# An encoder block on eight cores: x read transposed, 1/rms applied behind the projections, mixing and feed-forward over all 1024 tokens at once

## The chip, the cores and the metric

The kernel runs on all eight cores of one Trainium2 chip. Each core works alone on 1024 of the 8192 tokens, with its own copy of every weight, and the cores never exchange anything. The metric is the device time of the slowest core, in microseconds (us). A core has a matrix engine (TensorE, PE in the rows; PEld is its weight load), a vector engine (VectorE, DVE), an activation engine (ScalarE, ACT), GpSimd (POOL) and SyncE (SP). In this kernel POOL and SP only issue transfers: POOL those that turn f32 weights into bf16 on the way, SP the plain ones. Sixteen DMA engines move the bytes of both queues.

## The reference

```python
h = rms_norm(x, norm1_pre)                       # x: (2, 4096, 2048) f32
z = h @ w_in                                     # 2048 -> 7168: [u 1024 | v 1024 | p 1024 | ga 2048 | gb 2048]
u, v = gelu(z[u]), gelu(z[v]);  p = z[p]
y_a = u * (W_s @ layer_norm(v) + b)              # 8 heads, 128x128 matrix per block of 128 tokens
y_b = group_linear(trailing_mean(p, 2/4/8/16) - p) * scale     # needs 16 tokens of p before the first one
merged = sigmoid(ga) * (y_a @ w_a_out) + sigmoid(gb) * (y_b @ w_b_out)
x = x + rms_norm(merged @ w_mix_out, norm1_post)
h = rms_norm(x, norm2_pre)
x = x + rms_norm((silu(h @ w_ffn_gate) * (h @ w_ffn_up)) @ w_ffn_down, norm2_post)   # inner width 5632
```

## The kernel before

`Sched.add` records every operation with the bytes that it reads and writes; `analyze` and `emit` turn that into semaphore waits. Each engine runs its operations strictly in the order in which the program adds them, so the order of the code is the order of every queue. One byte array `arena` is the whole of SBUF, and buffers share addresses by hand. PSUM is eight banks of 128x512 f32; `nb()` hands them out in a circle. All matmuls are bf16, mostly 128x128 weights against 512 columns.

`stage_AB` takes the 1024 tokens once. Nine row tiles of x (16 halo tokens, then eight of 128) are loaded, squared and summed (L386), scaled by 1/rms (L395), transposed on PE (L349) and copied out of PSUM with the gain (L358, L362) into `hT`. Then come, each from `hT`:

- p (L448 halo, L460), eight chunks of 128 channels, evicted by ScalarE (L465); VectorE forms the trailing sums by one to four shifted adds of some 1039 columns (L475) and the mean minus the token (L482);
- v (L509), token tile by token tile, GELU (L514), layer norm on VectorE (L516 to L533), each tile with a square root on ScalarE;
- the pool's group linear (L549, evicted at L556), u with the 128x128 mixing (L572, L585), and the two gates with the two output projections (L623 to L632), 48 matmuls for each 128 output channels and 512 tokens, gathered in `mergedT`.

`stage_CDE(hf)` then runs twice, once for each half of 512 tokens:

- C: `mergedT @ w_mix` (L692), root mean square norm and residual (L738), second norm, transposes (L349 again) into `h2T`; the first three feed-forward slices run in halves of 256 columns between them (L766, L769);
- D: for each of 44 slices of 128 inner channels 16 + 16 matmuls (L807, L810), SiLU (L815) and product (L817), with a ring of three weight buffers of 1 MB;
- E: four blocks of 512 output channels, 44 x 4 matmuls each (L846), squares and gain (L855, L859); behind the fourth block all four token tiles are normed, added to x (L738) and stored (L866).

So `w_mix`, `w_gu` and `w_dn` are loaded twice, once for each half:

```python
        stage_AB()
        if last_stage in (None, "C", "D", "E"):
            for hf in range(nhalves):
                stat_ctr[0] = 128
                stage_CDE(hf)
```

Of the kernel before, what the change touches and what calls it, by code (L numbers as in the profile page):

```python
# [190 lines left out]
class Arena:  # L191
    def __init__(self, ap):
        self.ap = ap
        self.ptr = 0

    def alloc(self, nbytes, dtype, pattern=None, **kw):
        off = (self.ptr + GRAN - 1) // GRAN * GRAN if nbytes >= GRAN else (self.ptr + 31) // 32 * 32
        self.ptr = off + nbytes
# [4 lines left out]
        return v

def build_program(dbg=None, nhalves=2, last_stage=None):
    nc = bass.Bass("TRN2", target_bir_lowering=False)
# [31 lines left out]

    sems = []
    import contextlib  # L240
    with contextlib.ExitStack() as es:
# [4 lines left out]

# [32 lines left out]
        def dma(eng, out, in_, group=None, after=()):  # L279
            return S.add(eng, lambda e, o=out, i=in_: e.dma_start(out=o, in_=i),  # L280
                         reads=[in_], writes=[out], dma=True, group=group, after=after)

        def emit_consts(first_x_load):
            dma("sp", ident, ident_d, group="c0")
            dma("sp", g1T, g1T_d, group="c0")
            dma("sp", g2T, g2T_d, group="c0")
            dma("sp", pscT, pscT_d, group="c0")
            dma("sp", invf, invf_d, group="c0")
            dma("pool", sgwT, sgwT_d, after=[first_x_load])
            dma("pool", wpool, w_pool)  # L290
            S.add("dve", lambda e: e.memset(sgwT[64:128, :, 0:64], 0.0), reads=[], writes=[sgwT])
# [699 lines left out]
```

How the kernel before makes its waits and increments, by code:

```python
        def run(engname, e):  # L172
            waited = {}
            for op in per_eng.get(engname, []):
                need = {}
                for d in op.deps:
                    dop = self.ops[d]
                    if need.get(dop.sem, 0) < dop.sigval:
                        need[dop.sem] = dop.sigval
                for s, v in need.items():
                    if waited.get(s, 0) < v:
                        e.wait_ge(semh[s], v)
                        waited[s] = v
                if op.fn is None:
                    continue
                ins = op.fn(e)
                if op.signal:
                    ins.then_inc(semh[op.sem], 16 if op.dma else 1)
```

## Time and profile before

| | |
|---|---|
| median of 6 runs | 1733.83 us (1731.96 to 1734.46) |
| the profiled execution: its time | 1732.88 us |
| its span (slowest core, 5) | 1731.3 us |
| spans of the eight cores | 1718.7 to 1731.3 us |
| mean granted TensorE clock of the cores | 0.969 to 0.972 of full speed |
| PE busy | 1579.7 us, 91% |
| VectorE, ScalarE busy | 360.5 us (21%), 273.3 us (16%) |
| moved by the DMA engines | 226.14 MB, mean 131 GB/s |

The span runs from the first to the last instruction of a core; the profiled execution took 1.6 us more than its span. Busy shares are means over stages of very different kinds. DMA figures count the bytes that the transfers write; a weight that is cast on the way is read as twice as many bytes from HBM.

### The profile page before, as it was taken

What the parts mean: (1) busy time and instruction counts of PE and PEld (TensorE: products, weight loads), DVE (VectorE), ACT (ScalarE), POOL (GpSimd) and SP (SyncE); (2) the same over time, 40 slices, a digit from 0 to 9 for tenths busy, and PEclk for the clock granted to TensorE, in tenths of its full rate; (3) what the DMA queues carried; (4) which work ended last, traced back from release to release, by engine and by line L of the source; (5) the groups of instructions that cost most, each with busy time, mean ns of one, the idle gap of its engine ahead of it and who ended that gap; (6) DMA issues with size and microseconds to landing.
All of it is one profiled execution on the core that took longest, in us unless ns stands there. A gap on an engine that the chain in (4) does not pass through costs nothing.

```text
span 1731.3 us, 19473 instructions; the slowest of 8 cores (1718.7 to 1731.3 us)
## 1 busy us (share of the span) xinstructions
PE 1579.7 (91%) x7728; PEld 746.2 (43%) x7728; DVE 360.5 (21%) x654; ACT 273.3 (16%) x585; POOL 122.7 (7%) x234
## 2 busy tenths in 40 slices
PE   2699899999999986999999999986499999999994
PEld 1344344444444435444444444432344444444442
DVE  4366431112111233000100000041500110010003
ACT  6314411111111133000000000020400000000001
POOL 0000000000000000000000111100000000011110
PEclk9999999999999997999999999997789999999997
DMA  8950164444448760998899899999188888879992
GB/s 209 189 100 1 25 107 82 80 80 79 74 73 151 144 131 14 162 153 154 151 152 153 150 173 169 165 182 226 42 129 154 155 149 153 155 150 167 176 162 106
DMA packets 39258, 226.14 MB, mean 131 GB/s; under 512 B 4848, under 2 KB 6896, under 8 KB 21360
## 3 DMA queue, kind: packets, MB, share of 16 engines
q0 software_dynamic: 34528, 197.93, 68.1%
q1 hardware_dynamic: 4640, 26.96, 4.6%
q8 instruction: 63, 1.03, 0.2%
q14 instruction: 27, 0.22, 0.0%
HBM read 410.21 MB, written 8.39 MB: 242 GB/s over the span
## 4 chain that ended last, share of the span: by engine, by line
PE 85%; DMA 8%; DVE 3%; issue 2%; ACT 2%; DVEq 0%; POOL 0%; ACTq 0%; SPq 0%; POOLq 0%
PE psum L846 17%; PE psum L807 16%; PE psum L810 16%; PE psum L623 6%; PE psum L626 6%; DMA arena<-x_ext 4%; PE psum L460 3%; PE psum L692 3%; PE psum L509 3%; PE psum L632 3%; PE psum L629 3%; PE psum L572 3%; DMA out<-arena 1%; DMA arena<-w_dn 1%; PE psum L766 1%
## 5 line engine op out<-in xcount | busy, mean ns | idle before, releaser
L807 PE MATMUL psum<-arena 128*128 128x512 bf16 x1312 | 298.9, 381 | 8.0 <-DMA arena<-w_gu 8.0
L846 PE MATMUL psum<-arena 128*128 128x512 bf16 x1408 | 304.6, 379 | 1.4 <-DMA arena<-w_dn 1.3
L810 PE MATMUL psum<-arena 128*128 128x512 bf16 x1312 | 296.6, 379 | 0.0
L846 PEld LDWEIGHTS psum<-arena 128*128 128x128 bf16 x1408 | 137.3, 98 | 168.7 <-issue 4.0
L807 PEld LDWEIGHTS psum<-arena 128*128 128x128 bf16 x1312 | 128.9, 98 | 164.5 <-issue 11.8
L810 PEld LDWEIGHTS psum<-arena 128*128 128x128 bf16 x1312 | 128.3, 98 | 154.8
L817 DVE TENSOR_TENSOR arena<-arena,psum 128x512 bf16<-128x512 f32 x82 | 56.4, 688 | 521.5 <-ACT arena L815 521.5
L692 PE MATMUL psum<-arena 128*128 128x512 bf16 x512 | 112.7, 383 | 21.7 <-DMA arena<-w_mix 21.7
L815 ACT ACTIVATE arena<-psum 128x512 f32<-128x512 f32 x82 | 49.0, 597 | 528.5 <-PE psum L810 528.5
L623 PE MATMUL psum<-arena 128*128 128x512 bf16 x512 | 115.7, 379 | 0.9 <-DVE arena L592 0.9
L626 PE MATMUL psum<-arena 128*128 128x512 bf16 x512 | 115.7, 379 | 0.0
L349 PE MATMUL psum<-arena 128*128 128x128 bf16 (+1 forms) x272 | 27.3, 280 | 83.2 <-DVE arena L395 28.7
L280 POOL DMA_DIRECT2D arena<-w_gu x88 | 46.5, 529 | 715.4 <-PE psum L810 495.4
L692 PEld LDWEIGHTS psum<-arena 128*128 128x128 bf16 x512 | 50.5, 99 | 83.6 <-issue 24.5
L859 DVE TENSOR_TENSOR arena<-psum,arena 128x512 f32<-128x512 f32 x32 | 19.9, 683 | 289.7 <-ACT arena L855 289.7
L642 DVE TENSOR_TENSOR arena<-arena,psum 128x512 f32<-128x512 f32 x32 | 22.0, 688 | 267.1 <-ACT arena L638 267.1
L623 PEld LDWEIGHTS psum<-arena 128*128 128x128 bf16 x512 | 50.0, 98 | 61.3 <-issue 1.1
L626 PEld LDWEIGHTS psum<-arena 128*128 128x128 bf16 x512 | 50.1, 98 | 60.4
L855 ACT ACTIVATE arena<-psum 128x512 bf16<-128x512 f32 x32 | 18.6, 597 | 290.2 <-PE psum L846 290.2
L280 POOL DMA_DIRECT2D arena<-w_dn x88 | 46.5, 530 | 251.2 <-PE psum L846 211.5
L638 ACT ACTIVATE arena<-psum 128x512 f32<-128x512 f32 x32 | 19.1, 597 | 286.2 <-PE psum L632 286.2
L349 PEld LDWEIGHTS psum<-arena 128*128 128x128 bf16 (+1 forms) x272 | 23.8, 130 | 86.6 <-issue 86.5
(81 smaller groups left out, 1052.1 us busy)
## 6 DMA issues: line engine op xcount, KB each, us to landing
arena<-w_gu POOLq DMA_DIRECT2D x88, 1024.0 KB, 9.8
arena<-w_dn POOLq DMA_DIRECT2D x88, 512.0 KB, 11.3
arena<-w_gab POOLq DMA_DIRECT2D x16, 1536.0 KB, 12.9
arena<-x_ext SPq DMA_DIRECT2D x16, 1024.0 KB, 9.8
arena<-w_mix POOLq DMA_DIRECT2D x8, 2048.0 KB, 30.6
out<-arena SPq DMA_DIRECT2D x8, 1024.0 KB, 14.2
arena<-w_p POOLq DMA_DIRECT2D x8, 512.0 KB, 12.6
arena<-w_v POOLq DMA_DIRECT2D x2, 2048.0 KB, 24.9
```

Of the source, the lines that this page charges most:

```text
L280: return S.add(eng, lambda e, o=out, i=in_: e.dma_start(out=o, in_=i), reads=[in_], writes=[out], dma=True, group=group, after=after)
L460: ins = e.matmul(PS(b1), lhsT=slot[:, kc, :], rhs=hT[:, kc, hf * HT:(hf + 1) * HT], start=(kc == 0), stop=(kc == 15))
L509: ins = e.matmul(PS(b), lhsT=hT[:, kc, tb * 128:(tb + 1) * 128], rhs=Wv[:, ct, kc, :], start=(kc == 0), stop=(kc == 15))
L572: ins = e.matmul(PS(b1), lhsT=slot[:, kc, :], rhs=hT[:, kc, hf * HT:(hf + 1) * HT], start=(kc == 0), stop=(kc == 15))
L623: ins = e.matmul(PS(bs[0]), lhsT=slot[:, kc, :], rhs=hT[:, kc, tk], start=(kc == 0), stop=(kc == 15))
L626: ins = e.matmul(PS(bs[1]), lhsT=slot[:, 16 + kc, :], rhs=hT[:, kc, tk], start=(kc == 0), stop=(kc == 15))
L629: ins = e.matmul(PS(bs[2]), lhsT=slot[:, 32 + kc, :], rhs=yAT[:, kc, tk], start=(kc == 0), stop=(kc == 7))
L692: ins = e.matmul(PS(b), lhsT=mergedT[:, kc, tk0 + tb * 128: tk0 + (tb + 1) * 128], rhs=slot[:, kc, :], start=(kc == 0), stop=(kc == 15))
L807: ins = e.matmul(PS(b1), lhsT=slot[:, kc, :], rhs=h2T[:, kc, :], start=(kc == 0), stop=(kc == 15))
L810: ins = e.matmul(PS(b2), lhsT=slot[:, 16 + kc, :], rhs=h2T[:, kc, :], start=(kc == 0), stop=(kc == 15))
L817: S.add("dve", lambda e, b2=b2, o=sgj, f=f: e.tensor_tensor(out=hidT[:, f, :], in0=o, in1=PS(b2), op=ALU.mult), reads=[sgj, PS(b2)], write ...
L846: ins = e.matmul(PS(banks[tb]), lhsT=hidT[:, fc, tb * 128:(tb + 1) * 128], rhs=slot[:, fl, :], start=(fc == 0), stop=(fc == NFC - 1))
```

## The change

x is no longer transposed on PE. The host hands it over as `xTa` (512 tokens) and `xTb` (the other 512 and, last, the 16 halo tokens) in channel-major form, beside the plain `x` for the residual. `x_chunk` loads 128 channels, multiplies them by the gain into `xg` (bf16, not normed), squares them on ScalarE into one buffer `sq`, and adds them on VectorE to `acc`. The mean over channels is a matmul: `tok_rstd` gives 1/rms for each token of a tile as a column (for v, as the scale of the GELU), and three f32 matmuls with `ones` give it as a row on all partitions (`rsb`), by which VectorE multiplies every result of p, u and the gates as it leaves PSUM.

The order becomes v, p, u with the pool's linear between the heads, gates. v runs first, chunk by chunk as `w_v` (now 16 loads of 128 channels) and x arrive; the second half of x is processed between the evictions of the first half's v.

C, D and E run once over 1024 tokens: all of `w_mix` stays in four buffers, each `w_gu` slice serves two groups of 512 columns out of a ring of five, and each `w_dn` piece serves all eight token tiles out of a ring of eleven, with one PSUM bank for each tile. x after the first sub-layer goes to DRAM (`x1_d`) and comes back for the last residual. E's last block runs tile by tile, so that each tile is normed and stored as it ends.

The core of the diff:

```diff
+        def x_chunk(half, kc):
+            n = HT if half == 0 else HT + HALO
+            t = xr[(half * 16 + kc) % NXR][:, 0:n]
+            dma("sp", t, (xTa_d if half == 0 else xTb_d)[kc], after=[w_ops[12]] if (half, kc) == (1, 0) else ())
+            ts(xg[:, kc, xcols[half]], t, g1T[:, kc:kc + 1], ALU.mult)
+            a = acc[:, xcols[half]]
+            if kc == 0:
+                act(AF.Square, a, t)
+            else:
+                for lo in range(0, n, HT):
+                    hi = min(lo + HT, n)
+                    act(AF.Square, sq[:, 0:hi - lo], t[:, lo:hi])
+                    tt(a[:, lo:hi], a[:, lo:hi], sq[:, 0:hi - lo], ALU.add)
...
+        def v_mm(tb, ct, kcs):
+            b = (tb % 4) * 2 + ct
+            tk = slice(tb * 128, (tb + 1) * 128)
...
+        def tok_rstd(half, b):
+            pe([(PS(b)[:, i:i + 1], acc[:, half * HT + i * 128: half * HT + (i + 1) * 128], one1, True, True)
+                for i in range(4)], [acc[:, half * HT:(half + 1) * HT], one1], [b])
+            r4 = rt[:, half * 4:half * 4 + 4]
+            ts(r4, PS(b)[:, 0:4], EPS, ALU.add)
+            act(AF.Sqrt, r4, r4)
+            recip(r4)
...
+        def v_evac(tb, ct):
+            b = (tb % 4) * 2 + ct
+            d = vg[tb][:, ct * 512:(ct + 1) * 512]
+            act(AF.Gelu, d, PS(b), scale=rt[:, tb:tb + 1])
...
+        def v_norm_r(half):
+            r4 = lnr[:, half * 4:half * 4 + 4]
+            act(AF.Sqrt, r4, r4)
+            recip(r4)
...
+        def v_norm(tb):
+            v = vg[tb]
+            ts(v, v, mvs[:, tb * 2:tb * 2 + 1], ALU.subtract, lnr[:, tb:tb + 1], ALU.mult)
+            tt(v, v, lng, ALU.mult)
+            tt(v_ln[:, tb, :], v, lnb, ALU.add)
...
+        KA, KE = 12, 4
+        late = list(range(KA, 16))
+        for kc in range(16):
+            x_chunk(0, kc)
+        order = [(tb, ct) for tb in range(4) for ct in range(2)]
+        for kc in range(KA):
+            for tb, ct in order[:7]:
+                v_mm(tb, ct, [kc])
+        for tb, ct in order[:2]:
+            v_mm(tb, ct, late)
+        tok_rstd(0, 7)
+        for tb, ct in order[2:7]:
+            v_mm(tb, ct, late)
+        v_mm(3, 1, list(range(16)))
+        for i, (tb, ct) in enumerate(order):
+            v_evac(tb, ct)
+            if i >= 1:
+                x_chunk(1, i - 1)
+        dma("sp", lng, lng_d, group="ln")
+        dma("sp", lnb, lnb_d, group="ln")
+        v_norm_r(0)
+        for kc in range(7, 16):
+            x_chunk(1, kc)
+            if kc >= 12:
+                v_norm(kc - 12)
...
+        order = [(tb, ct) for tb in range(4, 8) for ct in range(2)]
+        for tb, ct in order[:7]:
+            v_mm(tb, ct, list(range(KE)))
+        for kc in range(KE, KA):
+            for tb, ct in order[:7]:
+                v_mm(tb, ct, [kc])
+        tok_rstd(1, 7)
+        for tb, ct in order[:7]:
+            v_mm(tb, ct, late)
+            v_evac(tb, ct)
+        SEG = [(0, 347), (347, 694), (694, NT)]
+        bbs = [0, 1, 2]
+        for b, (lo, hi) in zip(bbs, SEG):
+            pe([(PS(b)[:, 0:hi - lo], ones, acc[:, lo:hi], True, True)], [ones, acc[:, lo:hi]], [b])
+        v_mm(7, 1, list(range(16)))
+        for b, (lo, hi) in zip(bbs, SEG):
+            ts(rsb[:, lo:hi], PS(b)[:, 0:hi - lo], EPS, ALU.add)
+        v_evac(7, 1)
+        act(AF.Sqrt, rsb, rsb)
+        recip(rsb)
+        v_norm_r(1)
+        bank_ctr[0] = 3
+
...
+        for i, c in enumerate(pcs):
+            g = c // 2
+            w = 2 << g
+            slot = pslots[i]
+            pj = pTs[i % 2]
+            for lo, hi in SEG:
+                b = nb()
+                pe([(PS(b)[:, 0:hi - lo], slot[:, kc, :], xg[:, kc, lo:hi], kc == 0, kc == 15) for kc in range(16)],
+                   [slot, xg[:, :, lo:hi]], [b])
+                hi_t = min(hi, TOK)
+                tt(pj[:, HALO + lo:HALO + hi_t], PS(b)[:, 0:hi_t - lo], rsb[:, lo:hi_t], ALU.mult)
+                if hi > TOK:
+                    tt(pj[:, 0:HALO], PS(b)[:, TOK - lo:hi - lo], rsb[:, TOK:NT], ALU.mult)
...
+            cur, lo, step, bi = pj, 0, 1, 0
+            while step < w:
+                nlo = lo + step
+                dst = sAB[bi]
+                tt(dst[:, nlo:NT], cur[:, nlo:NT], cur[:, nlo - step:NT - step], ALU.add)
+                cur, lo, step, bi = dst, nlo, step * 2, bi ^ 1
+            stt(pooledT[:, c, :], cur[:, HALO:], 1.0 / w, pj[:, HALO:], ALU.mult, ALU.subtract)
+            tt(t16, cur[:, HALO:2 * HALO], invf[:, g, :], ALU.mult)
+            tt(pooledT[:, c, 0:HALO], t16, pj[:, HALO:2 * HALO], ALU.subtract)
+            if norm_q:
+                v_norm(norm_q.pop(0))
...
+        def gab_load(d):
+            dma("pool", ringB[d % 3], w_gab[d])
...
+                tt(u_, PS(b1), rsb[:, tk], ALU.mult)
+                act(AF.Gelu, u_, u_)
...
+                tt(yAT[:, h, tk], t_, u_, ALU.mult)
...
+        for d in range(16):
...
+                for b, t_ in ((bs[0], sa[hf]), (bs[1], sb[hf])):
+                    tt(t_, PS(b), rsb[:, tk], ALU.mult)
+                    act(AF.Sigmoid, t_, t_)
+                tt(sa[hf], sa[hf], PS(bs[2]), ALU.mult)
+                tt(sb[hf], sb[hf], PS(bs[3]), ALU.mult)
+                tt(mergedT[:, d, tk], sa[hf], sb[hf], ALU.add)
+            if d + 3 < 16:
+                gab_load(d + 3)
+            if d in (0, 2, 4):
+                dma("pool", Wmix[d // 2], w_mix[d // 2])
+            if d == 13:
+                dma("pool", Wmix[3], w_mix[3])
+
...
+        dma("sp", xt[0], x_d[0:128, :])
...
+        for f in range(3):
+            dma("pool", ringD[f], w_gu[f])
...
+        def rstd_col(dst, src):
+            ts(dst, src, 1.0 / D, ALU.mult, EPS, ALU.add)
+            act(AF.Sqrt, dst, dst)
+            recip(dst)
...
+        def c_mm(tb, et):
+            b = nb()
+            tk = slice(tb * 128, (tb + 1) * 128)
+            pe([(PS(b), mergedT[:, kc, tk], Wmix[et][:, kc, :], kc == 0, kc == 15) for kc in range(16)],
+               [mergedT[:, :, tk], Wmix[et]], [b])
+            cols = slice(et * 512, (et + 1) * 512)
+            act(AF.Square, junk, PS(b), accum=cpart[tb % 2][:, et:et + 1])
+            tt(mo[:, cols], PS(b), gp1[:, cols], ALU.mult)
+
+        def c_chain(tb):
+            x_, r_ = xt[tb % 2], cs[tb % 2]
+            sum4(r_[:, 0:1], cpart[tb % 2])
+            rstd_col(r_[:, 1:2], r_[:, 0:1])
+            stt(x_, mo, r_[:, 1:2], x_, ALU.mult, ALU.add)
...
+            dma("sp", x1_d[rows, :], x_, writes=[("dram", "x1", tb)])
+            act(AF.Square, xb[tb % 2], x_, accum=r_[:, 2:3])
+            rstd_col(r_[:, 3:4], r_[:, 2:3])
+            stt(xb[tb % 2], x_, r_[:, 3:4], g2, ALU.mult, ALU.mult)
+            if tb + 2 < 8:
+                dma("sp", x_, x_d[(tb + 2) * 128:(tb + 3) * 128, :])
...
+        def c_tr(tb):
...
+                S.add("pe", tr, reads=[xb[tb % 2], ident], writes=[PS(b)])
+                dst = h2T[:, half * 8:half * 8 + 8, tb * 128:(tb + 1) * 128]
+                src = pb.rearrange("p (c n) -> p c n", c=8)
...
+        for tb in range(8):
...
+                c_mm(tb, et)
+                if et == 1 and tb >= 2:
+                    c_tr(tb - 2)
+            c_chain(tb)
...
+        def d_mm(f, hf):
+            slot = ringD[f % NRD]
+            tk = slice(hf * HT, (hf + 1) * HT)
+            b1, b2 = nb(), nb()
+            for b, k0 in ((b1, 0), (b2, 16)):
+                pe([(PS(b), slot[:, k0 + kc, :], h2T[:, kc, tk], kc == 0, kc == 15) for kc in range(16)],
+                   [slot, h2T[:, :, tk]], [b])
+            return f, tk, b1, b2
...
+        def d_ev(f, tk, b1, b2):
+            s_ = sg[sgc[0] % 2]
+            sgc[0] += 1
+            act(AF.Silu, s_, PS(b1))
+            tt(hidT[:, f, tk], s_, PS(b2), ALU.mult)
...
+        def d_load(f):
+            dma("pool", ringD[f % NRD], w_gu[f])
...
+        pend = [d_mm(0, 0)]
+        c_tr(6)
+        pend.append(d_mm(1, 0))
+        pend.append(d_mm(2, 0))
+        d_ev(*pend.pop(0))
+        c_tr(7)
+        for p_ in pend:
+            d_ev(*p_)
+        d_load(3)
+        d_load(4)
+        for f in range(3):
+            d_ev(*d_mm(f, 1))
+            d_load(f + 5)
+        for f in range(3, NFC):
+            for hf in range(2):
+                d_ev(*d_mm(f, hf))
+            if f + 5 < NFC:
+                d_load(f + 5)
...
+        def e_load(i):
+            et, fg = eslots[i]
+            dma("pool", ringE[i % NRE], w_dn[et, fg])
...
+        for et in range(3):
+            cols = slice(et * 512, (et + 1) * 512)
+            for fg in range(11):
...
+                for tb in range(8):
+                    tk = slice(tb * 128, (tb + 1) * 128)
+                    pe([(PS(tb), hidT[:, fg * 4 + fl, tk], slot[:, fl, :], fg == 0 and fl == 0, fg == 10 and fl == 3)
+                        for fl in range(4)], [hidT[:, fg * 4:fg * 4 + 4, tk], slot], [tb])
+                    if fg == 10:
+                        act(AF.Square, junkE, PS(tb), accum=epart[tb][:, et:et + 1])
+                        tt(fo[:, tb, cols], PS(tb), gp2[:, cols], ALU.mult)
+                e_load(i + NRE)
+        for tb in range(8):
...
+            for fg in range(11):
+                slot = ringE[(33 + fg) % NRE]
...
+            act(AF.Square, junkE, PS(tb), accum=epart[tb][:, 3:4])
+            r_, x_ = es_[tb % 2], x1t[tb % 2]
...
+            rstd_col(r_[:, 1:2], r_[:, 0:1])
...
+            stt(x_[:, 0:512], f4, r_[:, 1:2], x_[:, 0:512], ALU.mult, ALU.add)
+            stt(f4, PS(tb), r_[:, 1:2], gp2[:, 1536:2048], ALU.mult, ALU.mult)
+            tt(x_[:, 1536:2048], f4, x_[:, 1536:2048], ALU.add)
+            stt(x_[:, 512:1536], fo[:, tb, 512:1536], r_[:, 1:2], x_[:, 512:1536], ALU.mult, ALU.add)
+            dma("sp", out_d[rows, :], x_, writes=[("dram", "out", tb)])
+            if tb + 2 < 8:
+                nrows = slice((tb + 2) * 128, (tb + 3) * 128)
+                dma("sp", x_, x1_d[nrows, :], reads=[("dram", "x1", tb + 2)])
```

## Rows read from the trace of the kernel before

**Rows 1.** The page's first line: span and slowest core.

```profile
span 1731.3 us, 19473 instructions; the slowest of 8 cores (1718.7 to 1731.3 us)
```

**Rows 2.** Timeline of PE: start, us, engine, line, instructions, idle before.

```profile
1239.16 1.91 PE L766 MATMUL psum<-arena 128*128 128x256 bf16 x16
1240.91 1.91 PE L769 MATMUL psum<-arena 128*128 128x256 bf16 x16
...
1246.15 1.06 PE L349 MATMUL psum<-arena 128*128 128x128 bf16 x16
...
1270.71 5.98 PE L807 MATMUL psum<-arena 128*128 128x512 bf16 x16 [4.10 <-DMA arena<-w_gu]
...
1556.98 152.11 PE L846 MATMUL psum<-arena 128*128 128x512 bf16 x704 [0.56 <-DMA arena<-w_dn]
```

**Rows 3.** Stretches: busy us of each engine, granted clock, DMA share, GB/s.

```profile
0.00:64.00 64.00, 15.39 (x147) 13.70 (x148) 26.73 (x92) 37.22 (x95) 4.58 (x12) 1.00 0.90 207
...
179.00:194.00 15.00, 9.78 (x33) 3.39 (x31) 8.41 (x12) 11.65 (x19) 0.00 (x0) 0.77 0.00 0
...
254.00:585.70 331.70, 331.53 (x1537) 150.33 (x1538) 62.02 (x95) 34.94 (x63) 11.15 (x21) 1.00 0.52 89
...
641.00:697.00 56.00, 31.20 (x257) 25.72 (x256) 22.73 (x59) 21.57 (x55) 1.59 (x3) 0.76 0.14 23
697.00:983.00 286.00, 285.37 (x1322) 129.29 (x1323) 28.21 (x41) 24.48 (x41) 23.58 (x45) 1.00 0.90 154
983.00:1134.00 151.00, 150.56 (x698) 67.77 (x696) 7.45 (x12) 7.26 (x24) 23.60 (x44) 1.00 1.02 168
...
1160.00:1215.00 55.00, 31.07 (x136) 13.36 (x133) 8.65 (x17) 6.69 (x21) 0.00 (x0) 0.81 0.99 229
1215.00:1271.00 56.00, 31.79 (x257) 26.06 (x258) 22.49 (x59) 20.62 (x53) 1.58 (x3) 0.74 0.19 38
...
1709.00:1731.30 22.30, 0.08 (x1) 0.00 (x0) 13.02 (x20) 4.51 (x13) 0.00 (x0) 0.58 0.46 188
```

**Rows 4.** DMA issues: KB each, median us to landing.

```profile
arena<-w_gu POOLq DMA_DIRECT2D x88, 1024.0 KB, 9.8
```

**Rows 5.** VectorE's groups by form: busy us, mean ns, idle before.

```profile
L738 DVE SCALAR_TENSOR_TENSOR arena<-arena 128x2048 f32<-128x2048 f32 x16 | 37.0, 2344 | 3.3 <-DMA arena<-x_ext 3.3
...
L642 DVE TENSOR_TENSOR arena<-arena,psum 128x512 f32<-128x512 f32 x32 | 22.0, 688 | 267.1 <-ACT arena L638 267.1
...
L516 DVE BATCH_NORM_STATS2 arena<-arena 128x6 f32<-128x512 f32 x16 | 10.2, 682 | 0.0
...
L395 DVE TENSOR_SCALAR arena<-arena 128x2048 bf16<-128x2048 f32 x8 | 10.2, 1278 | 0.0
L475 DVE TENSOR_TENSOR arena<-arena 128x1039 f32<-128x1039 f32 x8 | 9.9, 1242 | 25.9 <-ACT arena L465 25.9
...
L527 DVE TENSOR_SCALAR arena<-arena 128x1024 f32<-128x1024 f32 x8 | 6.5, 812 | 0.9
...
L333 DVE TENSOR_SCALAR arena<-arena 128x1 f32<-128x1 f32 x32 | 4.8, 149 | 6.0 <-ACT arena L386 5.2
```

**Rows 6.** ScalarE's groups by form, same columns.

```profile
L702 ACT ACTIVATE arena<-psum 128x512 bf16<-128x512 f32 x32 | 19.0, 596 | 92.2 <-PE psum L692 92.2
...
L744 ACT ACTIVATE arena<-arena 128x2048 bf16<-128x2048 f32 x8 | 15.2, 1898 | 0.2
L514 ACT ACT_TABLE_LOAD x8 | 10.3, 1283 | 1.1 <-PE psum L509 0.9
```

**Rows 7.** Timeline of one square root between two VectorE instructions.

```profile
637.95 0.15 DVE L333 TENSOR_SCALAR arena<-arena 128x1 f32<-128x1 f32 x1
638.19 0.20 ACT L336 ACTIVATE arena<-arena 128x1 f32<-128x1 f32 x1 [3.21 <-DVE arena L333]
...
638.49 0.16 DVE L338 RECIPROCAL arena<-arena 128x1 f32<-128x1 f32 x1 [0.40 <-ACT arena L336]
```

**Rows 8.** Timeline of SyncE's last DMA issues.

```profile
1719.63 7.11 SPq L866 DMA_DIRECT2D out<-arena  x4
```

More of the change, by code:

```diff
@@ L23 @@
 ARENA_BYTES = 212736
+NT = HALO + TOK
 GRAN = 256
@@ new lines, in build_program @@
+        acc = at(Z3 + 18 * KB + 512, F32, NT)
+        ones = at(Z3 + 23 * KB, F32, 128)
+        Z4 = Z3 + 24 * KB
+        sgwT = at(Z4, BF16, 8, 128)
+        wpool = at(Z4 + 2 * KB, BF16, 4, 2, 256)
+        sq = at(Z4 + 6 * KB, F32, HT)
+        sa = [at(Z4 + 2 * i * KB, F32, HT) for i in range(2)]
+        sb = [at(Z4 + (4 + 2 * i) * KB, F32, HT) for i in range(2)]
+        rsb = at(Z4 + 8 * KB, F32, NT)
+        Z5 = Z1 + 38 * KB
+        xt = [at(Z1 + (8 + 8 * i) * KB, F32, D) for i in range(2)]
@@ L277, in st @@
             return stat[:, o:o + n]
[L279 to L291, printed above, removed]
@@ new lines, in ts, with tt @@
+        def ts(out, in0, s1, op0, s2=None, op1=None):
+            kw = {} if op1 is None else {"op1": op1}
+            rd = [in0] + [s for s in (s1, s2) if hasattr(s, "tensor")]
+            return S.add("dve", lambda e: e.tensor_scalar(out=out, in0=in0, scalar1=s1, scalar2=s2, op0=op0, **kw),
+                         reads=rd, writes=[out])
+        def tt(out, a, b, op, eng="dve"):
+            return S.add(eng, lambda e: e.tensor_tensor(out=out, in0=a, in1=b, op=op),
+                         reads=[a, b], writes=[out])
@@ new lines, in pe, with fn @@
+        def pe(mms, reads, banks):
+            def fn(e):
+                ins = None
+                for o, l, r, s_, t_ in mms:
+                    ins = e.matmul(o, lhsT=l, rhs=r, start=s_, stop=t_)
+                return ins
+            return S.add("pe", fn, reads=reads, writes=[PS(b) for b in banks])
+        rt = st(8)
+        mvs = st(16)
+        lnr = st(8)
+        bst = [st(12) for _ in range(4)]
+        xcols = [slice(0, HT), slice(HT, NT)]
+        dma("act", g1T, g1T_d)
+        S.add("dve", lambda e: e.memset(ones, 1.0 / D), writes=[ones])
@@ new lines, in build_program @@
+        S.add("dve", lambda e: e.memset(one1, 1.0 / D), writes=[one1])
+        w_ops = [dma("pool", Wv[:, kc, :], w_v[kc]) for kc in range(16)]
+        def x_chunk(half, kc):
[11 more added lines that the diff above has]
+                    tt(a[:, lo:hi], a[:, lo:hi], sq[:, 0:hi - lo], ALU.add)
@@ new lines, in build_program, with wtile @@
+        v_norm_r(0)
[3 more added lines that the diff above has]
+                v_norm(kc - 12)
+        dma("sp", ident, ident_d, group="c1")
+        dma("sp", pscT, pscT_d, group="c1")
+        dma("sp", invf, invf_d, group="c1")
+        ra = [0]
+        def wtile(src):
+            slot = ringA[ra[0] % 4]
+            ra[0] += 1
+            dma("pool", slot, src)
+            return slot
+        pcs = [7, 6, 5, 4, 3, 2, 1, 0]
+        pslots = [wtile(w_p[c]) for c in pcs[:4]]
@@ new lines, in build_program @@
+        eslots = [(et, fg) for et in range(4) for fg in range(11)]
+        def e_load(i):
+            et, fg = eslots[i]
+            dma("pool", ringE[i % NRE], w_dn[et, fg])
+        for i in range(NRE):
+            e_load(i)
+        dma("sp", gp2, gp2_d)
+        epart = [st(4) for _ in range(8)]
+        es_ = [st(2) for _ in range(2)]
+        for tb in range(2):
+            rows = slice(tb * 128, (tb + 1) * 128)
+            dma("sp", x1t[tb], x1_d[rows, :], reads=[("dram", "x1", tb)])
```

768 lines of the change are left out of this document (187 added, 581 removed).

## The prediction

> **What bounds the kernel now.** The first line gives the span, 1731.3 us, and the slowest core [rows 1]. I read PE's timeline next. Where PE runs without a break, 704 matmuls of 512 columns take 152.11 us [rows 2]: 0.216 us each. Counted from the code, the program has 7072 such matmuls (v, p and u 256 each, the pool 32, gates and output projections 1536, C 512, D 2816, E 1408), 1528 us at that pace. So 203 us of the span are something else, and the table of stretches shows where [rows 3]. In the first 64 us PE works 15.4 us, on transposes. In 179 to 194 it is a third idle, waiting for the pool's evictions. In each half's stretch between C and D (641 to 697, 1215 to 1271) it works 31 to 32 of 56 us, and the DMA engines stand almost still: the chain of norms is the limit there. In 1160 to 1215 it works 31 of 55 us with the DMA engines at 0.99: the second half's `w_mix` and x. In the last 22.3 us it works not at all. In the long stretches it is full (331.53 of 331.70, 285.37 of 286.00) at a granted clock of 1.00. The bound is PE, and what can be won is the 203 us around it.
>
> **The second loads of the weights.** D and E load 154 and 168 GB/s with the DMA engines at 0.90 and 1.02 [rows 3], and yet PE loses 0.6 us in the 286 of D. The traffic that goes is hidden today, so halving it is worth nothing in these stretches. D's cover even grows: a slice feeds 64 matmuls, 13.8 us, against 9.8 us to land [rows 4].
>
> **PE's work after the change.**
> - v: 256 x 0.216 = 55.3 us.
> - p: 3 x 16 matmuls of 346 or 347 columns for each of 8 chunks. 16 of 256 columns take 1.75 us (two starts in [rows 2]), 0.109 each; between that and 0.216 a matmul of 347 costs 0.147: 8 x 48 x 0.147 = 56.6 us.
> - u and pool: 288 x 0.216 = 62.2, and 16 groups of four 128-column mixings at 0.066 (16 transposes in 1.06 us [rows 2]), 4.2: 66.4 us.
> - gates 331.8, C 110.6, D 608.3, E 304.1 us; eight tiles' transposes (16 each) 8.5 us.
> Together 1541.6 us. No transposes for the first norm, no halo matmuls.
>
> **The start, until v is done.** `w_v` and the first half of x are 4.19 MB each. At 168 GB/s (E's casts) and 229 GB/s (1160 to 1215) [rows 3] they take 25.0 + 18.3 us on the shared engines; from 2 us on, the last chunk lands at 45. Both at 229 it is 39, both at 168 it is 52. PE uses each chunk as it lands and is not the limit. What follows is a chain through VectorE, which runs in program order:
> - Chunk 15 squared (0.60, [rows 6]), added (0.69), four f32 matmuls (not in the trace; 0.6 taken, hundredths at the least), 1/rms with two handovers of 0.1 (the square root leaves VectorE idle 0.40 for 0.20 of work, [rows 7]), GELU's table load 1.28 and the first GELU 0.60 [rows 6]: 49.8.
> - Then evictions of v and chunks of the second half take turns. A chunk's gain costs 0.43 (between 0.149 for 1 column and 1.278 for 2048, [rows 5]), its adds 0.69 and 0.17. With `bn_stats` 0.68 and the aggregates that is 2.2 us a step. But `sq` is one buffer and 528 columns are two squares, so ScalarE may not write the 16-column square before the first add has read, nor the next chunk's before the second add. A step is then 16-column square 0.2, GELU 0.6, `bn_stats`, aggregates and gain 1.3, add 0.69 and three handovers: 3.1 us. Seven steps and the first `bn_stats`: 22.4, to 72.2.
> - Layer norm's root with a table load, VectorE waiting: 1.9. Chunks 7 to 11 at 2.06 (0.60, 0.69, 0.20, 0.17 and four handovers): 10.3. Chunks 12 to 15 at 1.7, with three `v_norm` of 0.81 + 2 x 1.24 between them [rows 5], under which the next square hides: 16.7. `acc` is complete at 101.1.
> - `tok_rstd(1)` stands ahead of the remaining matmuls in PE's queue, so PE waits for all this. Then 0.6, 28 matmuls 6.1, 2.5 for the half-rate clock after the idle (16 matmuls took 5.98 us instead of 3.46, [rows 2]), the three `ones` matmuls 0.9 (0.4 at full clock), and the last tile's 16 matmuls 3.5: v ends at 114.7.
> That is 59.4 us of loss, against 64 now. If the handovers on `sq` cost nothing it is 12 less.
>
> **p and u.** VectorE now evicts p: for each chunk 3 x 0.51 and the halo 0.18, the shifted adds at 1.24 [rows 5], the mean 1.24, two small ones 0.35, and `v_norm` 3.29 behind the first four. Wide windows first: 2 x 11.5 + 2 x 10.2 + 2 x 5.8 + 2 x 4.5 = 64.0 us against PE's 56.6. Ahead of it stands the row form of 1/rms, PE already running: GELU 0.7, table load 1.28, root 1.0, reciprocal of 1040 columns. That is not in the trace: at least an add's 1.24; at most 15.7, if the 15 ns by which a reciprocal of one column exceeds a `tensor_scalar` of one [rows 5, 7] were for each column. I take 1.24, since a one-column instruction is nearly all fixed cost. PE may run eight banks, 18.8 us, ahead; followed bank by bank it waits 3.0 us near the end of p, and 15.9 with the long reciprocal. In the Trainium skill, "VectorE: DVE Perf Modes", section "Walkthrough: the 8-slice pipeline in each mode", reciprocal repeats its divide step 8 times. As an estimate from that page it would take 8.7 us here and the sum would rise by 6 us; no run here shows it.
> In u VectorE has 6 x 0.69 = 4.1 us for each head against PE's 8.3, so it catches up. The gates add two multiplies to each group: 5 x 0.69 = 3.4 us against 48 matmuls, 10.4 us. These cost nothing; the cover is PE's own work, three times as long.
>
> **C, D, E.** For each tile VectorE has four evictions 2.8, two short roots 2.0, the residual and the scaling 2.34 each [rows 5], a wait for ScalarE's square of x 2.3 [rows 6], and the transposes' copy, 1.2: 12.9 us against PE's 13.8 + 1.06. It keeps up, and the eight banks bridge its latency. The plain x loads and x1 stores are 1 MB a tile each way, 4.6 us each at 229 GB/s, in 14.9. Around the last transposes (tile 7's behind three feed-forward groups) PE waits for one copy and a handover: 1.5. Changes of banks and late `w_dn` pieces in E: 1.5. At the end only one tile is left: square and root 2.0, four VectorE steps 3.3, the store from issue to end 4.6 (the last one now leaves at 1726.7, [rows 1, 8]): 10 instead of 22.3.
>
> **The sum.** 114.7 + (1541.6 - 55.3) + 3.0 + 1.5 + 1.5 + 10 = 1617.0 us of span. Cross-check by what goes: start 4.6, halo 3, pool 8, the stretches around C some 86, the tail 12: 114 off 1731.3. The profiled execution took 1.6 more than its span, 1732.9, and the median of the runs is 1.0 above that: **1620 us**.
>
> **Rivals.**
> - The handovers at the start are cheaper, or the loads faster: 1620 - 12 = 1608, and 6 less with the early landing, 1602. For it: only VectorE's own time is a floor. Against: one `sq`.
> - VectorE's queue is longer than its rows: the long reciprocal (+13) and the late landing (+7): 1640. For it: p's 64.0 against 56.6 leaves no room. Against: the eight banks.
> - C does not keep up: `mo` and the chain are one buffer deep for eight tiles, and 12.9 stands against 14.9. If the chain's 10 us behind a tile's last matmul were exposed half, 8 x 5 more: 1660.
> - Slower than before: the clock. Today PE's full stretches are broken up; afterwards it is full for some 1490 us. If the granted level fell to half, a matmul would cost 0.21 us more, and 540 of them, a stretch of 230 us at 1.2 GHz, use up the gain: 1734 and beyond. Against it: on all eight cores 331.7, 286 and 151 us went by at 1.00 [rows 3], and the clock fell only behind PE's idle time. The Trainium skill, "TensorE: Matmul & The Clock Gate", Part 1, warns that dense matmuls on several cores of a die lower its clock; by that rule the whole sum would grow, and this trace does not agree.
>
> **Chances and range.** Forecast, 1610 to 1632: 0.55. Cheaper start: 0.17. Longer VectorE queue: 0.17. C not keeping up: 0.08. Clock: 0.03. The range 1600 to 1645 takes in the first three. Faster by more than 0.2% (what a measurement of this kernel can tell from no change): 0.96; within it 0.01; slower 0.03.
>
> **What would show it.** PE idle some 15 us before the f32 matmuls of the second half, released by VectorE's add; VectorE near full from 50 us to the end of p; gates starting near 240 us; no gap of more than 3 us from there to the end of E; the end 10 us behind PE's last matmul. Wrong: a gap in every tile of C, a granted clock under 0.95 in D, or v done before 95 or after 130 us.

## The result and the profile after

| | before | after |
|---|---|---|
| median of the runs, us | 1734.27 (20 runs) | 1632.37 (10 runs) |
| after / before | | 0.9416, 95% interval 0.9405 to 0.9427 |
| profiled execution, us | 1732.9 | 1630.6 |
| its span, us | 1731.3 | 1629.1 |

The times and ratios here and below are those of executions in which no die was held at a lower clock than the other (in the others the mean granted clock of a die's cores was as low as 0.81), except that the two medians are over all runs. Forecast were 1620 us and a span of 1617.0; the direction is right, the time lies in the range, and the span is 12.1 us above the sum. Most of what follows is about these 12 us.

The page of the changed kernel, first lines and busy times: PE's share is now 96%.

```profile
span 1629.1 us, 18914 instructions; the slowest of 8 cores (1625.4 to 1629.1 us)
...
PE 1559.5 (96%) x7414; PEld 721.8 (44%) x7414; DVE 453.0 (28%) x694; ACT 230.9 (14%) x438; POOL 75.3 (5%) x146
```

Its stretches, read as [rows 3]:

```profile
45.00:67.00 22.00, 14.73 (x52) 6.78 (x52) 7.72 (x20) 7.00 (x13) 0.00 (x0) 0.73 1.02 205
...
89.00:107.50 18.50, 0.12 (x1) 0.00 (x0) 15.65 (x23) 3.39 (x8) 0.00 (x0) 0.58 0.01 2
107.50:125.20 17.70, 17.63 (x80) 9.65 (x81) 10.69 (x24) 8.93 (x12) 0.00 (x0) 0.86 0.09 30
125.00:185.00 60.00, 51.27 (x324) 32.51 (x322) 53.71 (x63) 0.49 (x2) 3.28 (x7) 0.94 0.37 71
...
250.00:582.00 332.00, 332.00 (x1546) 150.74 (x1544) 111.21 (x163) 43.25 (x68) 9.50 (x18) 1.00 0.57 100
...
700.00:1313.00 613.00, 612.06 (x2861) 278.41 (x2859) 69.73 (x102) 59.32 (x99) 26.91 (x51) 1.00 0.45 86
1313.00:1617.00 304.00, 304.00 (x1410) 137.75 (x1408) 44.32 (x74) 24.01 (x70) 17.96 (x34) 1.00 0.47 102
1617.00:1629.10 12.10, 2.11 (x10) 0.78 (x8) 3.87 (x7) 0.89 (x3) 0.00 (x0) 0.81 0.35 143
```

From 250 us to the end of E, PE is idle for less than 1 us in all, at a granted clock of 1.00, the 2.4 GHz level: the gaps around C, between the halves and in the pool [rows 3] are gone. The DMA share in D and E is 0.45 and 0.47, where it was 0.90 and 1.02. What is left lies before 185 us and in the last 10.

PE's waits (us in total, times, longest), and PE's timeline at the start (start, us, ..., idle before and its releaser):

```profile
PE psum L365 <- DMA arena<-w_v: 23.6, 12, 8.6
PE psum L365 <- DMA arena<-invf: 18.4, 1, 18.4
PE psum L365 <- DVE arena L347: 8.7, 3, 3.7
PE psum L365 <- DVE arena L343: 7.9, 4, 6.8
PE psum L365 <- DVE arena L645: 0.9, 1, 0.9
```

```profile
45.65 14.73 PE L365 MATMUL psum<-arena 128*128 128x512 bf16 x52 [7.30 <-DMA arena<-w_v]
67.22 15.84 PE L365 MATMUL psum<-arena 128*128 128x512 bf16 x63 [6.84 <-DVE arena L343]
...
107.57 47.71 PE L365 MATMUL psum<-arena 128*128 128x1 f32 x282 [18.45 <-DMA arena<-invf]
158.33 7.24 PE L365 MATMUL psum<-arena 128*128 128x346 bf16 x48 [3.05 <-DVE arena L347]
169.25 8.92 PE L365 MATMUL psum<-arena 128*128 128x346 bf16 x48 [3.67 <-DVE arena L347]
```

The wait of 18.45 us is the one for 1/rms of the second half. It is put down to the load of `invf`, but that load only ended last: VectorE's final add into `acc`, in the timeline below, begins at 105.90. The three waits that follow, 8.7 us, are p's matmuls waiting for banks that VectorE has not evicted.

VectorE's timeline, same columns:

```profile
53.73 1.29 DVE L413 BATCH_NORM_STATS2 arena<-arena 128x6 f32<-128x512 f32 x2 [2.16 <-ACT arena L337]
...
60.49 0.49 DVE L343 TENSOR_SCALAR arena<-arena 128x528 bf16<-128x528 f32 x1 [3.85 <-PE psum L365]
...
105.90 0.17 DVE L347 TENSOR_TENSOR arena<-arena 128x16 f32<-128x16 f32 x1 [0.41 <-ACT arena L337]
```

And its groups by form in 125 to 205 us, the stretch of p (as [rows 5]):

```profile
L347 DVE TENSOR_TENSOR arena<-arena 128x1039 f32<-128x1039 f32 x8 | 9.9, 1242 | 1.0 <-DVE arena L347 0.3
L352 DVE SCALAR_TENSOR_TENSOR arena<-arena 128x1024 bf16<-128x1024 f32 x8 | 9.8, 1225 | 1.4 <-DVE arena L347 1.4
...
L356 DVE RECIPROCAL arena<-arena 128x1040 f32<-128x1040 f32 x1 | 6.7, 6654 | 1.1 <-ACT arena L337 1.1
```

The reciprocal of 1040 columns took 6.65 us, where the sum had 1.24.

### The profile page after: what moved, and what is told of

Read it like the earlier page. It is cut to its first block, busy times and chain, and to the rows that moved or that the text cites. A ratio compares the mean times of both kernels' runs of the same rounds, so it can differ in the third digit from the quotient of the medians.

```text
span 1629.1 us, 18914 instructions; the slowest of 8 cores (1625.4 to 1629.1 us)
## 1 busy us (share of the span) xinstructions
PE 1559.5 (96%) x7414; PEld 721.8 (44%) x7414; DVE 453.0 (28%) x694; ACT 230.9 (14%) x438; POOL 75.3 (5%) x146
## 4 chain that ended last, share of the span: by engine, by line
PE 91%; DVE 4%; DMA 2%; issue 1%; ACT 1%; POOL 0%; DVEq 0%; ACTq 0%; SPq 0%; POOLq 0%
PE psum L365 90%; DVE arena L347 3%; DMA arena<-w_v 2%; ACT arena L337 1%; DVE arena L343 1%; POOL arena L326 0%; PE psum L635 0%; DVE arena L352 0%; DVE arena L413 0%; DVEq L183 0%; DMA arena<-invf 0%; DVEq L748 0%; DVE arena L645 0%; DVE arena L416 0%; ACTq L183 0%
## 5 line engine op out<-in xcount | busy, mean ns | idle before, releaser
L365 PE MATMUL psum<-arena 128*128 128x512 bf16 (+2 forms) x7286 | 1553.5, 376 | 59.6 <-DMA arena<-w_v 23.6
L365 PEld LDWEIGHTS psum<-arena 128*128 128x128 bf16 x7286 | 714.2, 99 | 895.0 <-issue 80.6
L347 DVE TENSOR_TENSOR arena<-arena,psum 128x512 bf16<-128x512 f32 (+1 forms) x152 | 104.4, 687 | 594.8 <-PE psum L365 594.3
L347 DVE TENSOR_TENSOR arena<-psum,arena 128x512 f32<-128x512 f32 (+3 forms) x168 | 106.2, 640 | 415.2 <-PE psum L365 383.9
L337 ACT ACTIVATE arena<-psum 128x512 f32<-128x512 f32 (+1 forms) x152 | 90.6, 597 | 853.7 <-PE psum L365 852.4
L337 ACT ACTIVATE arena<-arena 128x512 f32<-128x512 f32 (+3 forms) x164 | 95.4, 584 | 432.7 <-DVE arena L347 354.1
L347 DVE TENSOR_TENSOR arena<-arena 128x512 bf16<-128x512 f32 (+8 forms) x153 | 109.2, 714 | 28.5 <-ACT arena L337 19.4
L352 DVE SCALAR_TENSOR_TENSOR arena<-arena 128x1024 bf16<-128x1024 f32 (+4 forms) x40 | 63.7, 1592 | 5.1 <-DVE arena L356 3.0
L326 POOL DMA_DIRECT2D arena<-w_gu x44 | 23.2, 528 | 675.6 <-PE psum L365 518.7
L343 DVE TENSOR_SCALAR arena<-arena 128x1 f32<-128x1 f32 (+3 forms) x72 | 26.9, 376 | 38.8 <-ACT arena L337 18.1
L356 DVE RECIPROCAL arena<-arena 128x1 f32<-128x1 f32 (+2 forms) x29 | 11.2, 388 | 15.4 <-ACT arena L337 15.4
L635 PEld LDWEIGHTS psum<-arena 128*128 128x128 bf16 x128 | 7.8, 98 | 1.9
```

Source lines behind the costliest of these rows:

```text
L326: return S.add(eng, lambda e: e.dma_start(out=out, in_=in_), reads=[in_] if reads is None else reads, writes=[out] if writes is None else ...
L337: return S.add("act", lambda e: e.activation(out=out, in_=in_, func=func, **kw), reads=rd, writes=[out] + ([accum] if accum is not None el ...
L343: return S.add("dve", lambda e: e.tensor_scalar(out=out, in0=in0, scalar1=s1, scalar2=s2, op0=op0, **kw), reads=rd, writes=[out])
L347: return S.add(eng, lambda e: e.tensor_tensor(out=out, in0=a, in1=b, op=op), reads=[a, b], writes=[out])
L352: return S.add("dve", lambda e: e.scalar_tensor_tensor(out=out, in0=in0, scalar=scalar, in1=in1, op0=op0, op1=op1), reads=rd, writes=[out])
L356: S.add("dve", lambda e: e.reciprocal(out=x_, in_=x_), reads=[x_], writes=[x_])
```

## The experiments

**Theory A**: from 50 us to the end of p, VectorE's queue (its work and its waits) is the bound. What leaves it, or a wait of its that goes, moves everything after it; what is only moved within it gives nothing. **Rival B**: only PE's wait for the second half's 1/rms costs; whatever brings that forward is a gain in full. Spans, each of the slowest core, are compared with 1629.1; the eight cores of that one execution differ by 3.7 us, so differences of 1 or 2 us are not read.

**e1: finer tracking of what instructions share.** The scheduler orders accesses by pieces of `GRAN` bytes. A row of `xg` has 2080 bytes, so the columns that VectorE writes for the second half share a piece with columns that PE still reads for the first: the 3.85 us at 60.49. `pscT`, `one1` and `g1T` share one too.

```diff
-GRAN = 256
+GRAN = 32
```

> Dependencies are tracked in pieces of 32 bytes instead of 256; nothing else changes. In the trace of the changed kernel VectorE stands still 3.9 us at 56.6 us until PE has ended the first half's last v matmuls (rows of xg are 2080 bytes apart, so the columns that VectorE writes and those that PE reads share a piece), and PE starts the f32 matmuls 1.5 us after the last add, behind three small transfers that share a piece with a constant. Theory A (VectorE's queue, waits included, sets the time from 50 us to the end of p): both waits go, 4 to 5 us less, 1627 us, ratio 0.997. Theory B (PE's wait for 1/rms of the second half alone costs, VectorE has slack in p): 5 us less at the end of v as well, so this run doesn't tell A from B. Theory C (the waits are cover for something else, as the landing of x): under 1 us.

Measured: 1627.1 to 1627.5 us in three executions and 1636.5 in a fourth (the changed kernel, too, has one of 1640.1 beside 1630.1 to 1634.0), ratio 0.9395 (0.9371 to 0.9418), span 1625.6. VectorE's gain runs without the wait, and PE's row of the second 1/rms in the trace of e1 is

```profile
102.32 48.66 PE L365 MATMUL psum<-arena 128*128 128x1 f32 x281 [16.63 <-DVE arena L347]
```

It is 5.25 us earlier, now put down to VectorE's add, and the span gains 3.5. Both false waits were real: they cost 5.25 us at the start, of which 3.5 reach the end. The ratio's interval overlaps that of the changed kernel, so the verdict rests on the rows.

**e2: a second `sq` buffer**, so that a square does not wait for the add ahead.

```diff
-        sq = at(Z4 + 6 * KB, F32, HT)
+        sq = [at(Z4 + (6 + 2 * i) * KB, F32, HT) for i in range(2)]
```

> Two buffers for the squares instead of one. Theory A: a step of eviction and chunk falls from 2.9 to about 2.3 us (seven of them), a chunk alone from 2.1 to 1.4 (five), a chunk with layer norm by 0.4 (four): 9 us less, 1623 us, ratio 0.9945, and PE's wait in p stays at 8.7 us. Rival: the handovers are hidden by VectorE's own work: under 2 us.

Measured: 1622.7 to 1625.3 us, ratio 0.9356 (0.9342 to 0.937), span 1621.4. The f32 matmuls start at 97.80 instead of 107.57, and p's waits stay at 8.8. The single buffer cost 9.8 us at the start (the first rival had 12), of which 7.7 reach the end.

**e3: layer norm of v's first four tiles behind the second 1/rms.** This is the run that tells A from B: four layer norms, 13 us of VectorE's work, go behind it, and three of them, 10 us, stood ahead of the last add into `acc`.

```diff
             x_chunk(1, kc)
-            if kc >= 12:
-                v_norm(kc - 12)
...
         tok_rstd(1, 7)
+        for tb in range(4):
+            v_norm(tb)
```

> The layer norm of the first four v tiles moves behind the square root for the second half's tokens, so that the sum of squares is complete three layer norms, 10 us, earlier. Theory A (VectorE's queue up to the end of p is the bound, wherever its work stands): v ends about 10 us earlier on PE, and PE waits as much more in p; the time stays within 3 us, 1629 to 1633 us. Theory B (PE's wait for 1/rms of the second half is the cost): 8 to 10 us less, 1623 us, ratio 0.9945.

Measured: 1629.5 to 1630.8 us, ratio 0.9394 (0.9381 to 0.9406), span 1627.9. PE's timeline in e3, from the second 1/rms on:

```profile
98.38 41.62 PE L365 MATMUL psum<-arena 128*128 128x1 f32 x234 [9.26 <-DMA arena<-invf]
145.03 9.47 PE L365 MATMUL psum<-arena 128*128 128x346 bf16 x48 [5.04 <-DVE arena L347]
157.34 7.24 PE L365 MATMUL psum<-arena 128*128 128x346 bf16 x48 [2.84 <-DVE arena L347]
168.26 9.79 PE L365 MATMUL psum<-arena 128*128 128x346 bf16 x48 [3.67 <-DVE arena L347]
179.17 17.37 PE L365 MATMUL psum<-arena 128*128 128x346 bf16 x106 [1.12 <-DVE arena L347]
196.81 4.46 PE L365 MATMUL psum<-arena 128*128 128x512 bf16 x22 [0.27 <-DVE arena L347]
201.85 58.47 PE L365 MATMUL psum<-arena 128*128 128x512 bf16 x308 [0.58 <-DVE arena L347]
```

The wait for 1/rms fell from 18.45 to 9.26 us, the matmuls start 9.2 earlier, and v ends 8.2 earlier. All but 1.2 of that came back: PE's waits behind VectorE in p and u are 13.5 us instead of 8.7, and with the slower clock behind them p takes 5.5 us longer and u 1.5. B falls; the queue is the bound, not the place of the wait in it.

**e4: the long reciprocal left out.** p, u and the gates are scaled by the root itself instead of its reciprocal.

```diff
         act(AF.Sqrt, rsb, rsb)
-        recip(rsb)
```

> The reciprocal of the row form of 1/rms (1040 columns, 6.65 us on VectorE) is left out, so that p, u and the gates are scaled by the root itself. Theory A: PE's wait in p falls from 8.7 to about 3 us, 1626.5 us, ratio 0.9965. Rival: PE's eight banks hide it: no change, and the wait in p stays.

Measured: 1626.7 to 1628.2 us, ratio 0.9379 (0.9366 to 0.9391), span 1625.2. p's waits fell to 6.0, not to 3, and PE is through p 3.7 us sooner: less than the 6.65 us of work that went. In e4's timeline VectorE, free early, now waits for PE to fill p's first banks:

```profile
126.98 0.52 DVE L347 TENSOR_TENSOR arena<-psum,arena 128x347 f32<-128x347 f32 x1 [0.93 <-PE psum L365]
129.32 0.58 DVE L347 TENSOR_TENSOR arena<-psum,arena 128x330 f32<-128x330 f32 x2 [1.83 <-PE psum L365]
```

The remaining 6.0 belong to p's own evictions and sums, which take VectorE longer than PE needs for the matmuls. The reciprocal is only part of the miss in p.

**e5: D in two passes**, each slice of `w_gu` loaded twice, as before the change, with everything else of the change kept.

```diff
-            for hf in range(2):
-                d_ev(*d_mm(f, hf))
...
+        seq = [(f, hf) for hf in range(2) for f in range(NFC)]
+        for j in range(3, len(seq)):
+            d_ev(*d_mm2(j))
+            d_load2(j + 5)
```

> The changed kernel with D in two passes over the 512-column halves, each slice of the gate and up weights loaded twice again (88 loads of 1 MB instead of 44, a ring of five); the rest as changed, no norms between the passes. If the second loads were hidden before, as the prediction has it: the same time within 2 us, 1629 to 1632 us, with the DMA engines' share in D doubled to about 0.9. Rival (half the traffic is what made D and the rest faster): up to 1 us a slice, 44 us more.

Measured: 1636.1 and 1637.7 us, ratio 0.9435 (0.9418 to 0.9451), span 1634.6, 5.5 more (the ratio's interval overlaps that of the changed kernel; the rows decide). The stretch of D in e5, the one in which its clock falls, and PE's timeline at its start:

```profile
1000.00:1313.00 313.00, 311.47 (x1422) 141.90 (x1450) 30.96 (x45) 27.25 (x46) 27.56 (x52) 1.00 0.89 153
737.00:742.00 5.00, 4.44 (x11) 1.66 (x12) 0.00 (x0) 0.00 (x0) 0.00 (x0) 0.50 1.01 159
```

```profile
737.56 262.65 PE L365 MATMUL psum<-arena 128*128 128x512 bf16 x1179 [4.17 <-DMA arena<-w_gu]
```

One wait of 4.2 us as the ring is first refilled, when a slice feeds 32 matmuls (6.9 us) and lands in 8.9; behind it PE's granted clock is 0.50 for 5 us. After that the traffic is doubled, 0.89 of the DMA engines' time, and PE runs on. On the other seven cores the wait is 1.9 to 4.4 us. So loading `w_gu` once is worth some 5 us of the 102, at one place. The prediction had costed it at nothing; the expectation, too, missed this wait. No run loads `w_mix` or `w_dn` twice again. For `w_mix` the rows before speak of a cost: in 1160 to 1215 us, while the second half's `w_mix` and x came in, PE worked 31 of 55 us with the DMA engines at 0.99 [rows 3].

**f1: e1 and e2 together**, with both diffs above.

> Pieces of 32 bytes and two buffers for the squares together. Theory A (every wait in VectorE's queue before the end of p counts): the sum of the two alone, 12 us less than the changed kernel, 1619 us, v's f32 matmuls start near 93 us, PE's wait in p stays at 8.7 us. Rival (the two share what they remove, because ScalarE's handover and the false wait overlap): 8 to 9 us less, 1622 us.

Measured: 1620.3 us, ratio 0.9339 (0.9326 to 0.9351), span 1618.8. The two add up to 10.3 of the 11.2 us that they bring alone.

**f2: f1 with shorter work on VectorE.** The 16-column square and add go into the 512-column ones, layer norm takes two instructions for three, and 1/rms of 1040 columns is exp(-ln/2) on ScalarE.

```diff
-            ts(v, v, mvs[:, tb * 2:tb * 2 + 1], ALU.subtract, lnr[:, tb:tb + 1], ALU.mult)
-            tt(v, v, lng, ALU.mult)
-            tt(v_ln[:, tb, :], v, lnb, ALU.add)
+            stt(v, v, mvs[:, tb * 2:tb * 2 + 1], lng, ALU.subtract, ALU.mult)
+            stt(v_ln[:, tb, :], v, lnr[:, tb:tb + 1], lnb, ALU.mult, ALU.add)
...
-        act(AF.Sqrt, rsb, rsb)
-        recip(rsb)
+        act(AF.Ln, rsb, rsb)
+        act(AF.Exp, rsb, rsb, scale=-0.5)
```

> As the last one, with less work on VectorE up to the end of p: one square and one add for all 528 columns (0.5 us a chunk for sixteen), layer norm in two instructions instead of three (0.9 us a tile), and 1/root as exp(-ln/2) on ScalarE in place of the reciprocal (6.65 us). Theory A: by VectorE's work alone 5 us at the end of v (9 chunks at 0.3 and 3 tiles at 0.9) and PE's wait in p down from 8.7 to about 3: 1608 us. Rival (VectorE is no longer the bound once its waits are gone): no more than the 5 us at the end of v, 1614 us.

Measured: 1607.9 us, ratio 0.9266 (0.9254 to 0.9278), span 1606.3: the fastest of all, and 1.5% under the changed kernel. In f2's timeline of PE, the wait for 1/rms, two for p's evictions and one in u (sum of the last three 4.0):

```profile
90.81 56.08 PE L366 MATMUL psum<-arena 128*128 128x1 f32 x330 [7.39 <-DVE arena L348]
147.42 7.24 PE L366 MATMUL psum<-arena 128*128 128x346 bf16 x48 [0.53 <-DVE arena L348]
157.54 21.78 PE L366 MATMUL psum<-arena 128*128 128x346 bf16 x128 [2.89 <-DVE arena L348]
179.91 90.34 PE L366 MATMUL psum<-arena 128*128 128x512 bf16 x454 [0.58 <-DVE arena L348]
```

And VectorE now also waits for x, as at the second and third of such chunks:

```profile
58.22 0.49 DVE L344 TENSOR_SCALAR arena<-arena 128x528 bf16<-128x528 f32 x1 [1.05 <-DMA arena<-xTb]
62.04 0.49 DVE L344 TENSOR_SCALAR arena<-arena 128x528 bf16<-128x528 f32 x1 [1.72 <-DMA arena<-xTb]
```

**f3: f2 with two chunks of x behind each of v's evictions and all of layer norm inside p.** Layer norm of the first tiles then reads places into which p's sums and u's constants have already been written, so v's part of the output changes; the instructions are the same.

```diff
-            if i >= 1:
-                x_chunk(1, i - 1)
+            x_chunk(1, 2 * i)
+            x_chunk(1, 2 * i + 1)
...
-        norm_q = list(range(4, 8))
+        norm_q = list(range(8))
```

> As the last one, with the second half of x processed two chunks behind each eviction of the first half's v, and all eight layer norms behind the square root for the second half. Theory A: v's f32 matmuls start near 82 us and v ends near 100, but VectorE then has four more layer norms in p (10 us), so that PE waits more there: 8 to 12 us less than the last, near 1598 us. Theory B (PE's wait for 1/rms alone costs): 20 us less. If x lands too late for two chunks a step, no gain at all.

Measured: 1622.1 us, ratio 0.9347 (0.9335 to 0.9359), span 1619.7: 13.4 more than f2, a clear miss. From f3's timelines of VectorE and of PE:

```profile
61.46 0.49 DVE L344 TENSOR_SCALAR arena<-arena 128x528 bf16<-128x528 f32 x1 [3.02 <-DMA arena<-xTb]
```

```profile
187.30 82.96 PE L366 MATMUL psum<-arena 128*128 128x128 bf16 x411 [9.16 <-DVE arena L353]
```

VectorE runs in order. Chunks that have not landed now stand ahead of v's statistics, and PE waits 8.7 us for v's evictions; still, v ends 2.3 us earlier than in f2. But layer norm that was taken out of the queue's idle places comes back at its end, where u's mixing needs `v_ln`: 9.2 us, and the gates begin 13.4 us later than in f2. It fails for the reason that e3 showed: the work is moved, not taken out, and here to where PE waits for it.

## Why the prediction was right, and where it was off

**What bounds the kernel, and the halved traffic.** Right in kind: the 102 us of span came from the gaps around PE's work, from C on. The first line is the start of C in the chain of the kernel before; the second is ScalarE's first square of C in the trace after, 3.7 us behind the start of C:

```profile
585.85 55.27 PE psum L692 x256
```

```profile
592.23 0.60 ACT L337 ACTIVATE arena<-psum 128x512 bf16<-128x512 f32 x1 [5.48 <-PE psum L365]
```

From the start of C to PE's last matmul it was 1123 us (585.9 to 1709.1, [rows 2]) and is 1031 (588.5 to 1619.1): 93 of the 102 us, where the prediction had some 86. The end behind PE's last matmul gives 12, as costed. Everything ahead of C, with x read transposed and 1/rms behind the projections, loses some 3 us, where the prediction's terms put C's start at 572.5 and so had it win 13. No run separates the parts of the change from C on. e5 corrects one term: traffic was hidden in the steady part of D, as costed, but not in the ring's first refill, some 5 us.

**The start.** v ends on PE, and p begins, at 122.1 us, against 114.7 (+7.4); v's last eviction, which waits for its last matmul, starts just behind:

```profile
122.32 0.69 ACT L337 ACTIVATE arena<-psum,arena 128x512 f32<-128x512 f32 x1 [4.52 <-PE psum L365]
```

- The last chunk lands at 45.65 (45 costed). The first `bn_stats` is at 53.73 instead of 49.8: `late` matmuls of two banks, eight of them, stand ahead of `tok_rstd(0)`, and after 7.30 us of idle PE runs them at the 1.2 GHz level: the first six take 2.72 us, 0.45 each (granted clock 0.50 in 45.6 to 50.9, 0.73 in 45 to 67). The prediction left these eight out, some 3.4 us, and had the four f32 matmuls behind them at 0.6 instead of 1.7; in return the last chunk's square and add were not on the path, since x had landed ahead of `w_v`. Together +3.9.
- The seven steps end at 77.43: 23.7 us against 22.4. In them is the false wait of 3.85 us, which was not foreseen; the rest is 2.5 less than costed.
- From there to the last add, at 106.07, the costed chain fits: 28.6 us against 28.9.
- The load of `pscT` waits for an instruction that it has nothing to do with, the last chunk's gain; `invf` is issued behind it, and PE waits for both: 1.5 us, not foreseen.
- From the f32 matmuls to v's end, 14.5 us against 13.6. The one-column f32 matmuls take 1.8 us (0.6 costed), those with `ones` 2.0 (0.9 costed), and each is recorded as two instructions. The 28 behind the idle take 7.6 us, where 6.1 and 2.5 for the half-rate clock were costed: that term was 1 us too large.

PE's idle before these matmuls is 18.45 us, where some 15 were expected. VectorE was not near full there, as "what would show it" had it: it is busy 15.65 of 18.5 us in 89 to 107.5 and less before; its handovers and waits fill the rest, and e2 and e1 take part of them out.

So the start did not gain 4.6 us, as the cross-check had it, but lost 2.8: 122.1 less 55.3 of work is 66.8, against 64.

**p: the term that was off most.** From its first matmul at 122.1 to u's first at 191.3, p takes PE 69.2 us, against 59.6 costed (+9.6). PE waits 8.7 us, against 3.0, and its clock falls behind two of the three waits: 48 matmuls that take 7.24 us behind the first take 8.92 behind the second, and the 16 behind the third 4.19 instead of 2.51, 3.4 us in all. VectorE sets this length: on all eight cores p takes the same within 0.1 us, while PE's idle in it is 7.5 to 10.4. The direction (VectorE above PE's 56.6) was right. The reciprocal is 6.65 us, between the bounds 1.24 and 15.7, and the lower one was taken; without it p is 3.7 us shorter (e4). "VectorE: DVE Perf Modes" of the Trainium skill, section "Walkthrough: the 8-slice pipeline in each mode", gave an estimate of 8.7 and a sum 6 us higher; that was the better choice for the sum. By rows its price per column is 5.4 times that of an add (6654 ns for 1040, 1242 for 1039), not 8. Apart from the reciprocal, VectorE's work in p was right: the forms in 125 to 205 us add up to 63.8 us, 64.0 costed. But from its first eviction at 132.32 to the end it takes 69.7, because an instruction that has to wait for the one ahead starts 0.17 us behind its end, and because early on VectorE waits for PE once, 0.5 us. The sum had work and no waits.

**u, gates, C, D, E, the tail.** The gates begin near 257 us: 240.7 by the prediction's terms and the 17 us that are late at the end of p, less 0.7 in u. From C's start near 588.5 to PE's end at 1619.1 it is 1030.6 us, 1034.5 costed; PE waits there 0.9 once, where 3.0 were allowed. The end is 10.0 us behind PE's last matmul, as costed.

**The sum**: +7.4 at the start, +9.6 in p, -5 behind them, 12 in all; the profiled execution is 1.5 above its span. That the total is off by 12 and not by 17 is luck: allowances behind p that were not needed.

**The rivals.** The longer queue on VectorE came true in one of its two parts, the reciprocal, in part (+5.4 us of work where it had +13 of time), and in waits that it did not name; the late landing did not come. The cheaper start did not come by itself, but its mechanism is real: e2 makes it, and 9.8 us of its 12 are there. C keeps up. The clock stayed at 1.00 in 332, 613 and 304 us on end with all eight cores at work (the cores' means 0.983 to 0.986), so neither that rival nor the rule of "TensorE: Matmul & The Clock Gate", Part 1, of the Trainium skill, which weighed against the change, shows in this trace.

## What to carry to other kernels

Where one engine's queue runs in order, cost it with its handovers and false waits as well as its work, and count what stands ahead of each waiting instruction on the other engine too; moving work within a full queue only moves the wait (e3, f3), taking work or a wait out of it pays (e1, e2, f2). When the bound is an engine's idle time between stages, look for the gain there and not in halved traffic that was hidden, but check each ring's first refill. Read a change of several parts stage by stage: here the stages from C on gained 93 us and the end 12, while the stages ahead of C lost 3 until VectorE's queue was made shorter (f2). An instruction that the trace before lacks, on a path without slack, is sized between its bounds and not at the lower one.
